# A float32r weight stream: the split tiles that TensorE reads as the moving operand start 32 bytes later in their slots

## The reference, cut to what matters

```
h @ w_in, mem @ w_mem_kv, y @ w_up, m @ w_out
swiglu(x) = (silu(x @ w_gate) * (x @ w_up)) @ w_down      (hidden width 2816, four times)
mla: w_in, w_uq, w_ukv, w_o        nsa: w_in, w_o
```

## Time and profile before

| | |
|---|---|
| median of 3 runs | 1422.8 us |
| the profiled execution | 1423.93 us |
| its span, first to last instruction | 1422.1 us |
| TensorE matmul busy | 1409.4 us (99%), 8950 matmuls |
| TensorE weight load busy | 1276.1 us (90%) |
| VectorE / ScalarE / GpSimd busy | 925.0 / 741.1 / 62.9 us |
| granted TensorE clock, mean | 0.997 |
| read from HBM | 237.10 MB |

### The profile page before, as it was taken

The page is one execution under the profiler, slowest core; times in us unless marked ns, Lnnn a source line. Parts: engine busy times, 40 slices in busy tenths (PEclk is TensorE's granted clock), DMA queues, the critical chain, the costliest instruction groups (busy, mean ns, idle before and its releaser), DMA issues.

```text
span 1422.1 us, 23069 instructions
## 1 busy us (share of the span) xinstructions
PE 1409.4 (99%) x8950; PEld 1276.1 (90%) x8950; DVE 925.0 (65%) x1340; ACT 741.1 (52%) x1007; POOL 62.9 (4%) x89
## 2 busy tenths in 40 slices
PE   9999999999999999999999999999999999999998
PEld 8999999999988888899888888888889999888886
DVE  5555788675666656768666666666657578666656
ACT  6556673344355444558654545544545258554454
POOL 2000010010010000010120000100000000200000
PEclk9999999999999999999999999999999999999999
DMA  8444441255545555462375555755555400455552
GB/s 322 169 159 136 162 148 60 90 193 182 191 143 200 203 180 201 155 201 76 125 268 203 194 189 178 241 202 179 179 200 183 148 31 2 175 210 192 188 196 89
DMA packets 34630, 239.69 MB, mean 169 GB/s; under 512 B 3898, under 2 KB 4042, under 8 KB 6656
## 3 DMA queue, kind: packets, MB, share of 16 engines
q1 hardware_dynamic: 32832, 231.52, 46.6%
q0 software_dynamic: 1440, 6.67, 1.5%
q10 hardware_dynamic: 288, 0.52, 0.1%
HBM read 237.10 MB, written 1.08 MB: 167 GB/s over the span
## 4 chain that ended last, share of the span: by engine, by line
PE 95%; DVE 2%; ACT 1%; issue 1%; DMA 0%; SPq 0%; POOL 0%; POOLq 0%; ACTq 0%; DVEq 0%
PE ps L715 22%; PE ps L685 16%; PE ps L687 16%; PE ps L686 16%; PE ps L723 11%; PE ps L942 3%; PE ps L965 2%; PE ps L952 1%; PE ps L1228 1%; PE ps L2729 1%; PE ps L2737 1%; PE ps L624 1%; PE ps L2741 1%; PE ps L2904 1%; PE ps L806 1%
## 5 line engine op out<-in xcount | busy, mean ns | idle before, releaser
L392 DVE TENSOR_TENSOR low<-raw,high 128x2048 fp32r<-128x2048 f32 (+1 forms) x195 | 442.2, 2269 | 210.1 <-ACT high L386 207.8
L386 ACT ACTIVATE high<-raw 128x2048 fp32r<-128x2048 f32 (+2 forms) x198 | 374.0, 1891 | 44.1 <-PE ps L687 40.8
L715 PE MATMUL ps<-nt,high 128*128 128x512 f32 x1344 | 320.0, 390 | 0.0
L715 PEld LDWEIGHTS ps<-nt,high 128*128 128x128 f32 x1344 | 249.3, 188 | 50.6 <-issue 0.9
L685 PE MATMUL ps<-nt,high 128*128 128x256 f32 x656 | 186.9, 285 | 0.0
L686 PE MATMUL ps<-nt,high 128*128 128x256 f32 x656 | 185.6, 283 | 0.0
L687 PE MATMUL ps<-nt,low 128*128 128x256 f32 x656 | 185.6, 283 | 0.0
L723 PEld LDWEIGHTS ps<-nt,low 128*128 128x128 f32 x1344 | 167.1, 192 | 3.4
L723 PE MATMUL ps<-nt,low 128*128 128x256 f32 x1344 | 168.1, 283 | 0.0
L686 PEld LDWEIGHTS ps<-nt,high 128*128 128x128 f32 x656 | 125.9, 192 | 0.1
L685 PEld LDWEIGHTS ps<-nt,high 128*128 128x128 f32 x656 | 125.8, 192 | 0.1
(11 more groups left out here) (401 smaller groups left out, 2192.0 us busy)
## 6 DMA issues: line engine op xcount, KB each, us to landing
raw<-in_stream SPq DMA_DIRECT2D x216, 1024.0 KB, 4.9
late<-in_w POOLq DMA_DIRECT2D x1, 2048.0 KB, 9.7
scr<-bias_by_distance POOLq DMA_DIRECT2D x1, 2048.0 KB, 12.6
scr<-in_mem SPq DMA_DIRECT2D x2, 512.0 KB, 4.7
raw<-in_stream SPq DMA_DIRECT2D x4, 256.0 KB, 6.9
x<-in_x SPq DMA_DIRECT2D x1, 1024.0 KB, 12.5
con<-in_con SPq DMA_DIRECT2D x1, 592.0 KB, 12.8
row<-in_row SPq DMA_DIRECT2D x1, 592.0 KB, 14.1
```

The costliest lines, as they stand in the source:

```text
L386: nc.scalar.activation(high[t % SLOTS][:, 0:n], raw[t % SLOTS][:, 0:n], ACT.Copy).then_inc(w_high, 1)
L392: nc.vector.tensor_tensor(low[t % SLOTS][:, 0:n], raw[t % SLOTS][:, 0:n], high[t % SLOTS][:, 0:n].bitcast(F32), ALU.subtract).then_inc(w_l ...
L715: last = nc.tensor.matmul(r3(bank, 2), w[:, k, P * j:P * j + P], nt[:, :, k, :], start=first and k == 0, stop=not first and k == KC - 1, s ...
```

## The change

Each slot of `high` and `low` gets 16 more floats (64 bytes), so that it is 2064 floats long. A tile whose name is in `MOVING` is written and read 8 floats (32 bytes) further on in its slot; all others stay at its start. `raw` is unchanged. No instruction, wait or loop is added or removed. Each later allocation moves up by 6 x 64 = 384 bytes.

```diff
+HALF_LINE = 8
+MOVING = {f"f{f}d{i}" for f in range(4) for i in range(FT)} | {f"{n}{j}" for n in ("out", "mlao", "nsao") for j in range(4)} \
+    | {f"{n}{j}" for n in ("mv", "xmz", "swz", "gmv", "dnz") for j in range(2)} | {"uv", "nvs", "nvw"}
...
-        high = [sb(f"high{i}", [P, TW], F32R) for i in range(SLOTS)]
-        low = [sb(f"low{i}", [P, TW], F32R) for i in range(SLOTS)]
+        high = [sb(f"high{i}", [P, TW + 16], F32R) for i in range(SLOTS)]
+        low = [sb(f"low{i}", [P, TW + 16], F32R) for i in range(SLOTS)]
...
+        def place(t):
+
+            return HALF_LINE if PLAN[t] in MOVING else 0
...
-            nc.scalar.activation(high[t % SLOTS][:, 0:n], raw[t % SLOTS][:, 0:n], ACT.Copy).then_inc(w_high, 1)
+            at = place(t)
+            nc.scalar.activation(high[t % SLOTS][:, at:at + n], raw[t % SLOTS][:, 0:n], ACT.Copy).then_inc(w_high, 1)
...
         def slot(t, k, w):
-            return [h[t % SLOTS][:, 0:k * w].rearrange("p (k w) -> p k w", k=k) for h in (high, low)]
+            at = place(t)
+            return [h[t % SLOTS][:, at:at + k * w].rearrange("p (k w) -> p k w", k=k) for h in (high, low)]
```

More of the change, by code:

```diff
@@ L391, in split_low @@
             n = TW if i is not None else USED.get(PLAN[t], TW)
-            nc.vector.tensor_tensor(low[t % SLOTS][:, 0:n], raw[t % SLOTS][:, 0:n],
-                                    high[t % SLOTS][:, 0:n].bitcast(F32), ALU.subtract).then_inc(w_low, 1)
+            at = place(t)
+            nc.vector.tensor_tensor(low[t % SLOTS][:, at:at + n], raw[t % SLOTS][:, 0:n],
+                                    high[t % SLOTS][:, at:at + n].bitcast(F32), ALU.subtract).then_inc(w_low, 1)
         def split_low_half(dve, t, half):
@@ L398, in split_low_half @@
                 dve.wait_ge(w_high, t + 1)
-            c = slice(TW // 2 * half, TW // 2 * half + TW // 2)
-            ins = nc.vector.tensor_tensor(low[t % SLOTS][:, c], raw[t % SLOTS][:, c], high[t % SLOTS][:, c].bitcast(F32),
+            n = TW // 2
+            c, h = slice(n * half, n * half + n), slice(place(t) + n * half, place(t) + n * half + n)
+            ins = nc.vector.tensor_tensor(low[t % SLOTS][:, h], raw[t % SLOTS][:, c], high[t % SLOTS][:, h].bitcast(F32),
                                           ALU.subtract)
@@ L1579, in merge_split_high @@
             act.wait_ge(w_used, val(t - SLOTS + 1, by(i, 6)))
-            nc.scalar.activation(high[t % SLOTS][:], raw[t % SLOTS][:], ACT.Copy).then_inc(w_high, 1)
+            nc.scalar.activation(high[t % SLOTS][:, place(t):place(t) + TW], raw[t % SLOTS][:], ACT.Copy).then_inc(w_high, 1)
         def merge_split_low(dve, t, i):
             dve.wait_ge(w_high, val(t + 1, by(i, 6)))
-            nc.vector.tensor_tensor(low[t % SLOTS][:], raw[t % SLOTS][:], high[t % SLOTS][:].bitcast(F32),
+            nc.vector.tensor_tensor(low[t % SLOTS][:, place(t):place(t) + TW], raw[t % SLOTS][:],
+                                    high[t % SLOTS][:, place(t):place(t) + TW].bitcast(F32),
                                     ALU.subtract).then_inc(w_low, 1)
```

## The result

The changed kernel takes 1426.2 us in the median of 10 runs, the kernel before 1423.7 in 10 runs beside it. The ratio is 1.002 (95% interval 1.0011 to 1.0029): slower, by 2.6 us. I had forecast 4.0 us faster.

A forecast was written before the change was run, and what follows sets the result against it. It took TensorE's one long stream of matmuls, and their pitch, as the bound. Terms of -4.1, -0.2, -0.1 and +0.4 us made -4.0, so 1422.8 - 4.0 = 1418.8 us; range 1413 to 1425.

The forecast's parts named there:

- What bounds the kernel, and which matmuls count: TensorE busy 99% of the span at full clock; the change touches 1584 matmuls of 512 columns, 1056 in FFN down.
- The two cases: Half a line off in the earlier trace: moving yth, 2.1 to 3.4 ns lower pitch; stationary in uv, 6.9 ns higher.
- The pitch of the 1584: Matmuls with moving high or low, 512 columns: -2.6 ns each from 226.7 ns, together -4.1 us.
- The bound from uv: Upper bound for the 512-column pitch change, +6.9 ns, from tile uv's 233.6 ns against 226.7.
- Rival 2: At 512 columns, FFN down first, half a line keeps streams from settling: 10.9 us slower, 1433.7 us; chance 0.12.
- The floor of 216 ns: Best pitch of a full 512-column stream, taken from the float32 matmuls L2953; 10.7 ns below 226.7.
- rival 3: A large gain: the extra beyond the columns goes wholly or mostly, up to -16.9 us, 1405.9 us; chance 0.12.
- Rival 4: Slots 129 x 64 bytes apart move about half of 5,200 stationary-weight matmuls either way: 1410 to 1427 us; chance 0.06.
- nvs, nvw and uv: nvs and nvw, 96 matmuls of 256 columns: -0.2 us; uv, 24 matmuls: 0 to -0.2, taken as -0.1 us.
- The change of rhythm and the splits: Resettling when one stream follows another: 0 to +1.3 us, taken as +0.4; splits 32 bytes further on: hidden, 0.
- The rule of the Trainium skill: Warm pitch is columns / 2.4 + about 2.5 ns, so an address is worth nothing: sum 0, 1422.8 us.

The follow-up runs named there:

- m1: Not the kernel: 100 streams of 48 float32r matmuls, 256 or 512 columns, stationary and moving operand offset by 0 to 128 bytes; only pitches measured.
- e2: Kernel before plus only the half line: moving tiles 32 bytes on, slots 8448 bytes apart; 1433.2 us, ratio 1.0068.
- e1: Kernel before plus only the change's slot stride (2064 floats), no tile half a line off; 1422.2 us, ratio 0.9991.
- e7: e2 with hth and htl, the stationary operands of FFN down, half a line off too; 1428.5 us, ratio 1.0036 to the kernel before.
- e3: e2 with HALF_LINE = 0, so slots 8448 bytes apart and no tile half a line off; 1423.3 us, ratio 0.9998 to the kernel before.
- e4: Kernel before with only the three low slots 64 bytes further on; ratio 1.0004.
- m2: m1 with the moving operand fixed, the stationary one in steps of 16 bytes, and streams mixing two distances; only pitches measured.
- e5: e3's memory with only the low part of tiles that stay stationary 64 bytes further on; 1416.2 us, ratio 0.9957 to the kernel before.
- e8: e3's layout with each kind of tile's two parts placed by the grids of m1 and m2; 1407.3 us, ratio 0.9889 to the kernel before.
- e6: e5 with the high part of stationary tiles 64 bytes on too, except FFN gate and up; 1414.3 us, ratio 0.9935 to the kernel before.

## Why the prediction was wrong

- *What bounds the kernel, and which matmuls count.* Right: 99% TensorE, and but for 0.6 us of a wait the result lies in pitches. That "each slice of the granted clock is at full speed" read too much out of the earlier trace rows: a digit of 9 stands for 90% or more, and one slice hid 3.4 us at the 1.2 GHz level.
- *The step that failed: "So it isn't the distance between the two operands alone that counts, or both cases would have one sign."* The two cases were not alike. `yth` had 256 columns and uv 512, and I put the difference down to which operand was off. m1 shows that the side doesn't matter and the number of columns does. With that, uv was the right row for the change, and `yth` the wrong one.
- *The pitch of the 1584.* Forecast -2.6 ns, -4.1 us. In e2, where it stands alone, it is (371.9 - 362.7) / 1584 = +5.8 ns, +9.2 us. The bound from uv (+6.9) was good. "The gain at 256 columns should come once per matmul at 512 as well" had no row at 512 behind it but uv, which said the opposite. The sum got its sign from this term: the measured one is 13 us away from it (+9.2 against -4.1).
- *Rival 2, slower.* It named mechanism and place rightly, with 10.9 us for what e2 measures as 9.7. It had 0.12, because of the argument above. The floor of 216 ns, which stood behind rival 3, was reached by no float32r stream; none fell below 226.7.
- *Rival 4, the stride.* Real as well, and not a matter of 0.06. e1: 7.3 us of pitch lost at 512 columns and 8.4 gained at 256. Its sign had been named: L715 and L723 both changed, and of the 40 unbroken down blocks in after 30 take 5.55 us and 10 take 5.60. I had written that all stationary tiles were "still on a multiple of 64 bytes", and took that for harmless. The trace couldn't have told: every distance in it was a multiple of 256 bytes, or that and 32. The two edits don't add up, 9.7 - 1.3 is not 2.6: once the stride has spoiled the distance where weights move (+4.4 us of pitch), the half line adds only 3.0 more.
- *nvs, nvw and uv.* nvs and nvw gained 0.1 us where I had 0.2. uv fell in e2 from 233.6 to (651.50 - 648.96) / 11 = 230.9 ns, between the two ends I gave. Its pitches settle like those of e7's down: the second block of twelve has five in a row of 226 to 227 ns before its last, as distance 0 asks.
- *The change of rhythm and the splits.* The wide group behind down took 3.65 us instead of 3.62 in the kernel after, the upper end of my term. e2 shows the term by itself, as its wide tiles haven't moved: 307.7 us instead of 306.4, +1.3. The splits cost nothing that shows: VectorE and ScalarE are busy 925.3 and 741.2 us where they were 925.0 and 741.1, and TensorE's wait for a split is 1.0 us in both traces.
- *The rule of the Trainium skill* (page "TensorE: Matmul & The Clock Gate", section "Wait — 56ns, not 53.3ns?", a warm pitch of columns / 2.4 + about 2.5 ns) gives no term for an address. The trace doesn't agree with it for float32r with a weight load each: at 512 columns the lowest pitch is 226.7 ns, and e2 and e3, which differ in the 32 bytes alone, are 0.7% apart.

What stays open is why. In a stream that has only one distance, the distance gives the pitch, up to a choice between two rhythms at some of them. In streams that mix several (e4's down, the 512-column ones of e1) the pitch is not the mean of the grid's values, and I have no rule for it; where m2 ran the same mixture, the kernel is near it in e5 (117.8 and 117.8 ns) and e8 (113.6 and 113.3), and not in e6 (115.4 and 117.8). Whether the partner of a moving tile is its own stationary tile or the next one, whose load runs at the same time, m1 and e7 can't tell, as both have the same distance there. That the two operands' reads collide in SBUF fits, but no run shows it.

## What to carry to other kernels

Where float32r matmuls with a weight load each fill TensorE, the pitch depended on the distance between the starts of the stationary and the moving operand, modulo 256 bytes (256 and 0 gave the same pitches). Streams of 512 moving columns want distance 0, those of 256 want another (64 for the high part with 192 for the low one was the best here), so a shared buffer needs a place for each kind of tile, and padding by one 64-byte line changes every distance behind it. Before carrying a price from one stream to another, check that the number of columns is the same. Before reading a sum over a stream as pitch, take out its waits and look at the granted clock in windows of a few us.

## What the runs showed that I had not expected

- Distance alone moves a full stream by up to 7.7 ns at 512 columns (226.7 to 234.4) and 6.7 ns at 256 (113.3 to 120.0).
- A stream can have two steady rhythms at one distance: 113.3 and 117.8 ns at 256 columns (64 bytes), 226.7 and 233.3 at 512 (16 and 144 bytes). What ran before it plays a part.
- When a stream comes back to distance 0 behind another distance, it takes seven matmuls to settle (e7's down).
- One displaced matmul in three raised the pitch of the other two (e4: 231.7 ns over all 24).
